# Expert positions of 112 slots, and silu in place of sigmoid and a product

## What is computed

```python
logits = (xf @ router_w + router_b)                 # 512 x 32
top_val, top_idx = lax.top_k(logits, 4)
gates = softmax(top_val)
# for each expert e, for the tokens routed to it:
gu = xb @ mlp1_w[e] + mlp1_b[e]                     # 1024 -> 2048
gate, up = gu[..., ::2], gu[..., 1::2]
gate = minimum(gate, 7.0)
up = clip(up, -7.0, 7.0)
act = (up + 1.0) * gate * sigmoid(1.702 * gate)
y = act @ mlp2_w[e] + mlp2_b[e]                     # 1024 -> 1024
out[token] += y * gates[token, e]
```

## Time and profile before

| | |
|---|---|
| time, median of 3 runs | 1603.47 us (1601.67 to 1604.37) |
| span of the profiled execution | 1602.2 us |
| TensorE matmul / weight load busy | 97% / 78% |
| VectorE / ScalarE / GpSimd busy | 82% / 67% / 22% |
| expert stage | from about 447 us to 1583 us |
| L1932, L1935, L1960, L1965 (expert matmuls) | 4608 matmuls, mean 389 to 399 ns |
| L1754 (`lo`) on VectorE | 384 x 2288 ns |
| L1618 (`hi`) on ScalarE | 384 x 1919 ns |
| DMA | 465 MB; 372 to 391 GB/s in most slices of the expert stage |

### The profile page before, as it was taken

The page is one execution under the profiler, slowest core; times in us unless marked ns, Lnnn a source line. Parts: engine busy times, 40 slices in busy tenths (PEclk is TensorE's granted clock), DMA queues, the critical chain, the costliest instruction groups (busy, mean ns, idle before and its releaser), DMA issues.

```text
span 1602.2 us, 27288 instructions
## 1 busy us (share of the span) xinstructions
PE 1547.4 (97%) x10197; PEld 1254.4 (78%) x10198; DVE 1320.1 (82%) x1101; ACT 1068.4 (67%) x1014; POOL 347.6 (22%) x278
## 2 busy tenths in 40 slices
PE   6899999987899999999999999999999999999997
PEld 5677777765778888888888888888888888888885
DVE  5556565656498999999999999999999999999996
ACT  4635353434367777777777777777777777777774
POOL 7100000001145322212222212222222222221210
PEclk9999999998999999999999999999999999999999
DMA  6211111006399999999999999999999999999993
GB/s 198 57 54 41 54 41 54 15 2 224 153 390 367 375 391 383 385 381 361 385 379 377 386 383 377 375 372 378 371 383 376 381 380 372 372 374 373 384 375 134
DMA packets 99101, 465.30 MB, mean 290 GB/s; under 512 B 11408, under 2 KB 38192, under 8 KB 49760
## 3 DMA queue, kind: packets, MB, share of 16 engines
q1 hardware_dynamic: 86176, 429.59, 68.7%
q0 software_dynamic: 12864, 34.85, 8.3%
HBM read 448.51 MB, written 22.69 MB: 294 GB/s over the span
## 4 chain that ended last, share of the span: by engine, by line
PE 73%; DVE 2%; DMA 1%; ACT 0%; issue 0%; DVEq 0%; POOLq 0%
PE psum L1932 29%; PE psum L1960 14%; PE psum L1935 14%; PE psum L1965 7%; PE psum L1330 3%; PE psum L1922 2%; PE psum L1914 2%; DVE w_pieces_lo L1754 1%; PE psum L1948 1%; DMA xg<-h_rows,gath_i 0%; DMA w_pieces<-in_mlp_w 0%; PE psum L1346 0%; PE psum L1338 0%; DVE x L1876 0%; DMA w_pieces<-in_w_out 0%
## 5 line engine op out<-in xcount | busy, mean ns | idle before, releaser
L1754 DVE TENSOR_TENSOR w_pieces_lo<-w_pieces,w_pieces_hi 128x2048 fp32r<-128x2048 f32 x384 | 867.6, 2288 | 79.8 <-ACT w_pieces_hi L1618 79.7
L1618 ACT ACTIVATE w_pieces_hi<-w_pieces 128x2048 fp32r<-128x2048 f32 x384 | 736.1, 1919 | 220.5 <-PE psum L1935 154.1
L1932 PE MATMUL psum<-w_pieces_hi,xh 128*128 128x512 f32 x1024 | 284.3, 399 | 0.0
L1932 PE MATMUL psum<-w_pieces_hi,xl 128*128 128x512 f32 x1024 | 274.4, 390 | 0.0
L1935 PE MATMUL psum<-w_pieces_lo,xh 128*128 128x512 f32 x1024 | 274.2, 389 | 0.0
L1558 POOL DMA_INDIRECT sum_rows<-ys,this_i x30 | 143.6, 4786 | 418.2 <-ACT ys L1638 417.9
L1932 PEld LDWEIGHTS psum<-w_pieces_hi,xl 128*128 128x128 f32 x1024 | 192.2, 188 | 41.3
L1935 PEld LDWEIGHTS psum<-w_pieces_lo,xh 128*128 128x128 f32 x1024 | 192.2, 188 | 40.3
L1932 PEld LDWEIGHTS psum<-w_pieces_hi,xh 128*128 128x128 f32 x1024 | 185.3, 188 | 45.1 <-issue 11.3
L1960 PE MATMUL psum<-w_pieces_hi,ah 128*128 128x512 f32 x512 | 158.0, 390 | 0.1
L1960 PE MATMUL psum<-w_pieces_hi,al 128*128 128x512 f32 x512 | 157.7, 389 | 0.0
(11 more groups left out here) (366 smaller groups left out, 1901.9 us busy)
## 6 DMA issues: line engine op xcount, KB each, us to landing
w_pieces<-in_mlp_w SPq DMA_DIRECT2D x384, 1024.0 KB, 8.0
w_raw<-in_w_in SPq DMA_DIRECT2D x26, 512.0 KB, 4.1
w_pieces<-in_w_out SPq DMA_DIRECT2D x8, 512.0 KB, 9.2
sum_rows<-x POOLq DMA_DIRECT2D x5, 512.0 KB, 3.7
chunk_work<-in_x SPq DMA_DIRECT2D x4, 512.0 KB, 6.1
sc<-pall POOLq DMA_DIRECT2D x16, 128.0 KB, 4.0
x<-in_x SPq DMA_DIRECT2D x4, 512.0 KB, 13.6
h_rows<-w_pieces POOLq DMA_DIRECT2D x4, 512.0 KB, 2.9
```

The lines of the kernel that those rows point to most:

```text
L1618: nc.scalar.activation(hi[:, p % RING], raw[:, raw_slot(b, p)].rearrange("p r n -> p (r n)"), ACT.Copy).then_inc(s_hi, 1)
L1754: nc.vector.tensor_tensor(lo[:, p % RING], raw[:, raw_slot(b, p)].rearrange("p r n -> p (r n)"), hi[:, p % RING].bitcast(F32), ALU.subtrac ...
L1932: nc.tensor.matmul(bank(up_bank(b) + c), a[:, k, :], hi[:, p % RING, c * 512:(c + 1) * 512], start=False, stop=False)
```

## The change

1. Slots. Experts are put at places. Place 0 is expert 0; place 1 is the expert with the most rows among 1 to 29, which changes places with expert 1. These two places have 128 slots, all others 112 (`NARROW`). In the matmuls of the narrow places the stationary operand has 112 columns, and PSUM gets 112 rows. The order is found out on VectorE at the end of `route_vector`; SyncE reads the expert of a place from SBUF into a register before it issues its loads, and `pick_bias` takes its column from a table built there. The lists are read in two DMAs, one for the wide places and one for the narrow. Rounds are five instead of four (a further one runs only if needed).
2. Activation. ScalarE computes silu(1.702 gate) in place of sigmoid(1.702 gate). The product min(gate, 7) x up of VectorE is gone, and `activate` takes min(silu, its value at 7). The factor 1/1.702 that is then missing is put into the gates.
3. On TensorE the turns 2 and 3 are written out ahead of the loop, since they work on a wide expert's down projection.

```diff
-INDEXED = EXPERTS + 2
+WIDE = 2
+NARROW = 112
+LAST_COL, RANK_COLS = 3, 5
...
-SIG_MAX = float(1.0 / (1.0 + np.exp(-1.702 * 7.0)))
-ROUNDS = S // P
+ALPHA = 1.702
+SILU_MAX = float(ALPHA * 7.0 / (1.0 + np.exp(-ALPHA * 7.0)))
+ROUNDS = -(-S // NARROW)
+LIST_ROWS = ROUNDS * P * EXPERTS
...
-        "pick": (p % EXPERTS) == np.arange(TURNS)[None, :],
+        "pick": (p % EXPERTS) == 0,
+        "lane": p % EXPERTS,
+        "among": np.broadcast_to(np.where((c >= 1) & (c < EXPERTS - 2), EXPERTS - 1.0 - c, -1e6)[:, :EXPERTS], (P, EXPERTS)),
+        "to_one": np.broadcast_to(1.0 - np.arange(EXPERTS)[None, :], (P, EXPERTS)),
+        "wide_first": np.broadcast_to((P - NARROW) * (np.arange(EXPERTS)[None, :] == 0), (P, EXPERTS)),
...
-        nc.vector.memset(rank[:], -1e6)
+        nc.vector.memset(pick_at[:], 0.0)
...
-        nc.vector.tensor_tensor(rank[:, :, 0:EXPERTS], hidden[:], ranks, ALU.add)
-        nc.vector.tensor_tensor(rank[:, :, INDEXED - 1:INDEXED], hidden[:, :, EXPERTS - 2:EXPERTS - 1], ranks[:, :, EXPERTS - 2:EXPERTS - 1], ALU.add)
-        chain(nc.vector.memset(r1[:, 29:30], 0.0))
+        nc.vector.tensor_tensor(rank_at[:, :, 0:1], hidden[:, :, 0:1], ranks[:, :, 0:1], ALU.add)
+        chain(nc.vector.tensor_tensor(rank[:], hidden[:], ranks, ALU.add))
...
-        chain(nc.vector.tensor_reduce(r1[:, 20:21], bank(5, NT * EXPERTS, (NT + 1) * EXPERTS), AX.X, ALU.max))
+        counts = bank(5, NT * EXPERTS, (NT + 1) * EXPERTS)
+
+        def over_tokens(a):
+            return a.rearrange("p (t e) -> p t e", t=1).to_broadcast([P, NT, EXPERTS])
+
+        chain(nc.vector.scalar_tensor_tensor(largest[:], counts, float(EXPERTS), con("among"), ALU.mult, ALU.add))
+        chain(nc.vector.tensor_reduce(r1[:, 21:22], largest[:], AX.X, ALU.max))
+        chain(nc.vector.tensor_scalar(only[:], largest[:], r1[:, 21:22], None, ALU.is_equal))
+        chain(nc.vector.tensor_tensor_reduce(moved[:], only[:], con("experts"), 1.0, 0.0, ALU.mult, ALU.add, r1[:, 22:23]))
+        chain(nc.vector.tensor_tensor(moved[:], only[:], con("to_one"), ALU.mult))
+        chain(nc.vector.tensor_tensor(place_of_expert[:], moved[:], con("experts"), ALU.add))
+        chain(nc.vector.tensor_copy(place_of_expert[:, 1:2], r1[:, 22:23]))
+        nc.vector.tensor_scalar(gates[:], gates[:], 1.0 / ALPHA, None, ALU.mult)
+        for place in range(1, 3):
+            last = nc.vector.scalar_tensor_tensor(at_place[:, place - 1], over_tokens(place_of_expert[:]), float(place), rank[:], ALU.is_equal, ALU.mult)
+        chain(last)
+        nc.vector.tensor_copy(expert_at[:], place_of_expert[:]).then_inc(g["s_order"], 1)
+        nc.vector.tensor_scalar(pick_at[:, 0:EXPERTS], place_of_expert[:], con("lane"), None, ALU.is_equal).then_inc(g["s_order"], 1)
+        nc.vector.tensor_reduce(rank_at[:, :, 1:3].rearrange("p t n -> p n t"), at_place[:], AX.X, ALU.add)
+        nc.vector.tensor_copy(rank_at[:, :, LAST_COL:RANK_COLS], rank[:, :, EXPERTS - 2:EXPERTS])
+        chain(nc.vector.scalar_tensor_tensor(largest[:], only[:], float(NARROW - P), counts, ALU.mult, ALU.add))
+        chain(nc.vector.tensor_tensor(largest[:], largest[:], con("wide_first"), ALU.subtract))
+        chain(nc.vector.tensor_reduce(r1[:, 20:21], largest[:], AX.X, ALU.max))
         for r in range(ROUNDS):
-            last = nc.vector.tensor_scalar(flags[:, r:r + 1], r1[:, 20:21], float(P * r) if r else -1.0, None, ALU.is_gt)
+            last = nc.vector.tensor_scalar(flags[:, r:r + 1], r1[:, 20:21], float(NARROW * r) if r else -1e6, None, ALU.is_gt)
...
-            src = down_rows(d, b - 2, p) if p < DOWN else gate_up_rows(d, b, p - DOWN)
+            src = down_rows(d, e, p) if p < DOWN else gate_up_rows(d, e, p - DOWN)
...
+            sp.wait_ge(g["s_order"], 1)
+            e = expert(1)
             for p in range(DOWN, PIECES):
-                load(r, 1, p)
+                load(r, 1, p, e)
             with sp.Fori(2, EXPERTS) as b:
-                for p in range(PIECES):
-                    load(r, b, p)
+                e = expert(b - 2)
+                for p in range(DOWN):
+                    load(r, b, p, e)
+                e = expert(b)
+                for p in range(DOWN, PIECES):
+                    load(r, b, p, e)
...
-            nc.gpsimd.dma_start(lists[:, 0:EXPERTS, :], g["list_dram"].rearrange("(r s e) w -> r s e w", s=P, e=EXPERTS)[bass.ds(r, 1)].rearrange(
-                "a s e w -> (a s) e w")).then_inc(s_lists, 16)
-            pool.wait_ge(s_lists, r * 16 + 16)
+            rows = g["list_dram"].rearrange("(s e) w -> s e w", e=EXPERTS)
+            nc.gpsimd.dma_start(lists[:, 0:WIDE, :], rows[bass.ds(r * P, P), 0:WIDE, :]).then_inc(s_lists, 16)
+            nc.gpsimd.dma_start(lists[0:NARROW, WIDE:EXPERTS, :], rows[bass.ds(r * NARROW, NARROW), WIDE:EXPERTS, :]).then_inc(s_lists, 16)
+            pool.wait_ge(s_lists, r * 32 + 32)
...
-            nc.scalar.activation(sg[:], pairs(e)[:, :, 0], ACT.Sigmoid, scale=1.702).then_inc(s_sig, 1)
+            nc.scalar.activation(sg[:], pairs(e)[:, :, 0], ACT.Silu, scale=ALPHA).then_inc(s_sig, 1)
...
-            nc.scalar.activation(pick[:], con("pick")[:, bass.ds(m, 1)].to_broadcast([P, P]), ACT.Copy).then_inc(s_pick, 1)
+            if not isinstance(m, int) or m:
+                act.wait_ge(g["s_order"], 2)
+            column = con("pick") if isinstance(m, int) and not m else pick_at[:, bass.ds(m, 1)]
+            nc.scalar.activation(pick[:], column.to_broadcast([P, P]), ACT.Copy).then_inc(s_pick, 1)
...
-        def gate_up(r, e, b, p):
-
+        def clip_up(r, e, b, p):
             dve.wait_ge(s_used, r * STREAM + (place(b, p) + 1 + RING))
-            nc.vector.tensor_scalar(uu[:], pairs(e)[:, :, 1], 8.0, -6.0, ALU.min, ALU.max).then_inc(s_u, 1)
-            dve.wait_ge(s_u, r * EXPERTS + (e + 1))
-            nc.vector.scalar_tensor_tensor(uu[:], pairs(e)[:, :, 0], 7.0, uu[:], ALU.min, ALU.mult).then_inc(s_x, 1)
+            nc.vector.tensor_scalar(uu[:], pairs(e)[:, :, 1], 8.0, -6.0, ALU.min, ALU.max).then_inc(s_x, 1)
...
-            nc.vector.scalar_tensor_tensor(av[:], sg[:], SIG_MAX, uu[:], ALU.min, ALU.mult).then_inc(s_act, 1)
+            nc.vector.scalar_tensor_tensor(av[:], sg[:], SILU_MAX, uu[:], ALU.min, ALU.mult).then_inc(s_act, 1)
...
+        def width(b):
+            return P if isinstance(b, int) and b < WIDE else NARROW
+
+        def rows_of(n, width):
+            return bank(n, 0, 512, slice(0, width))
...
-                    nc.tensor.matmul(bank(up_bank(b) + c), a[:, k, :], hi[:, p % RING, c * 512:(c + 1) * 512], start=False, stop=False)
+                    nc.tensor.matmul(rows_of(at + c, m), a[:, k, 0:m], hi[:, p % RING, c * 512:(c + 1) * 512], start=False, stop=False)
...
-                    nc.tensor.matmul(bank(up_bank(b) + 2 * half + c), pick[rows, :], bias[rows, c * 512:(c + 1) * 512], start=True, stop=False)
-            if isinstance(b, int):
+                    nc.tensor.matmul(rows_of(up_bank(b) + 2 * half + c, width(b)), pick[rows, 0:width(b)], bias[rows, c * 512:(c + 1) * 512], start=True, stop=False)
...
-                        nc.tensor.matmul(bank(into + c), a[:, 2 * p + r2, :], hi[:, p % RING, r2 * D + c * 512:r2 * D + (c + 1) * 512],
+                        nc.tensor.matmul(rows_of(into + c, m), a[:, 2 * p + r2, 0:m], hi[:, p % RING, r2 * D + c * 512:r2 * D + (c + 1) * 512],
...
-            with pe.Fori(2, EXPERTS) as b:
+            for b in range(2, 2 + WIDE):
+                down(r, b)
+                up(r, b, True)
+            with pe.Fori(2 + WIDE, EXPERTS) as b:
```

89 lines of the change are left out of this document (53 added, 36 removed).

## The result

The changed kernel takes 1616.2 us (median of 4 runs, 1615.44 to 1616.78), the kernel before 1603.34 us in the same comparison: ratio 1.0079, 95% interval 1.0067 to 1.0092. I had forecast 1605.9 and a range up to 1609.5. The profiled execution spans 1614.2 us instead of 1602.2: 12 us are to be found, and 2.4 were expected.

A forecast was written before the change was run, and what follows sets the result against it. The prediction took TensorE as setting the pace, with the DMA engines also full. Its terms, -0.8 + 2.3 + 0.9 = +2.4 us, took the profiled 1602.2 to 1604.6, plus 1.3 for the median: 1605.9 us, range 1598.0 to 1609.5.

The forecast's parts named there:

- The stationary width: TensorE, 4320 matmuls of the narrow experts: 112 columns instead of 128 change nothing, 0; bounds 0 and 13.3 ns saved each.
- Rivals B and C: TensorE matmuls: B, load steals from the stream, -7.2 us, chance 0.10; C, load and matmul set spacing, 57 us, 0.08.
- The uncovered loads: TensorE, two weight loads per expert at and after the bias pair, each 13.3 ns shorter: -0.8 us.
- Silu and the product: VectorE loses 1.22 us per expert and gains only idle time, ScalarE's activation keeps its cost: 0.
- the cover: Slack before TensorE reads the piece behind the lists, done by 519.4 and read at 521.33: 1.9 us.
- The lists: Slot lists in two DMAs: one more issue costs about 0.6 us, its landing overlaps the first: 0 on TensorE.
- Rival D: Third expert: the second list DMA lands after the first, TensorE stands 2.3 us, result 1608.2; chance 0.20.
- The routing chain: VectorE between `stacked` and `select(0, 1)`, ahead of its first split: 4.1 us more, of which +2.3 us arrive.
- The end: Kernel's end: each engine checks one more round's flag, 0 to 1.5 us, taken as +0.9 us.

The follow-up runs named there:

- b_w112: Kernel before with only the width changed: stationary operand and result rows 112 wide for the experts in the loop; 1611.22 us, ratio 1.0048.
- a_list1: Changed kernel with the slot lists read by one transfer of 128 rows instead of two; 1614.13 us, ratio 1.0065.
- b_silu: Kernel before with silu in place of sigmoid, one product fewer on VectorE and a small scaling of the gates; 1605.33 us, ratio 1.0010.
- b_product: Kernel before with silu in place of sigmoid and a value-neutral product put back on VectorE; 1604.44 us, ratio 0.9997.
- a_nochain: Changed kernel without its routing operations, the order of the experts being a constant; 1614.94 us, ratio 1.0078.
- b_guard: Kernel before with one look at the second round's flag on each engine enclosing the loop over later rounds; 1603.81 us, ratio 0.9998.
- a_turns_product: Changed kernel with 128-column products, one list transfer, narrow experts' transposes over 112 rows and columns, and a product put back on VectorE; 1605.06 us, ratio 1.0006.
- a_best: a_turns_product with the guard of b_guard, and the last routing operations and flags moved behind the slot lists; 1602.9 us, ratio 0.9996.

## Why the prediction was wrong, step by step

**The stationary width: the step that failed.** I took 0 for 4320 matmuls, with bounds of 0 and a gain of 13.3 ns. The reading behind it was right as far as it went: a matmul without a load above it takes what it takes with one, so the load doesn't lengthen the stream. But I turned it into "width doesn't touch the spacing" and let a cost below zero out of the bounds, though no row of the trace had a stationary width other than 128 in this stream. Measured: 1.9 ns more per matmul in the mean of an expert (229.2 to 231.1, without the two groups of transposes but with what follows them), 0.26 us per expert, +7.6 us. Rivals B and C had the sign wrong: both supposed that less work can only be faster. The Trainium skill ("TensorE: Matmul & The Clock Gate", section "Back-to-back issue gap") has the spacing set by both the load and the matmul, and I had dismissed that; the runs don't contradict it, but less load is not less time, for at 112 columns the load is 14 ns shorter and the spacing 2.2 ns longer. That the cost comes by way of the load isn't shown: each of these edits narrowed the load, the matmul's own stationary side and its PSUM rows together, and none took them apart. The matmul ahead of a bias group, which has no load above it, hints that it isn't the load alone: the prediction had its 388 ns stay, and it lasts 397 with 112 columns (after and b_w112), 388 with 128 and with 88.

**The uncovered loads: mis-sized.** Forecast -0.8. From the last matmul ahead of a bias group to the first behind it went from 979 to 975 ns, not by 27: the bias matmul starts 327 ns after the last one instead of 318, and only what follows is shorter. Some 0.1 us in all.

**Silu and the product: the steady part right, the cover wrong.** "What VectorE gains is idle time" held in each steady expert: VectorE's idle time ahead of `lo` grew from 79.8 to 124.8 us. I didn't ask what the freed VectorE would run into: GpSimd's issues in the first three experts, +0.95 us on the last scatter.

**The lists: the place right, the cause wrong.** Rival D named the third expert, 2.3 us, and that is what it cost (2.27), but the number agrees by luck: a_list1 shows that the second transfer is 0.2 of it. The list arrives 4.1 us later, in three parts: the scatters' end (0.95), the wait for the last one's landing (5.08 to 6.04 us) and the slower transfer (4.8 to 7.0 us). Less a cover of 1.7 us, which I had put at 1.9, that is 2.4. Only the first part is traced to the change, by b_silu and b_product. The landing took 4.6 to 6.2 us over the seventeen kernels, and why it and the transfer were slow here is open.

**The routing chain: size near, place wrong.** 4.1 us forecast, 3.4 measured. I followed it through VectorE's splits to the second bias group and took +2.3. It surfaces ahead of the first transposes, by 0.6 to 0.8 us. The first split came at 443.89 and the second bias group at 472.06, for 445 and 473.3 forecast.

The first expert's +0.78 is two things in the traces. Behind the first bias group the granted clock is at 0.50 (1.2 GHz) for 1.20 us before and 2.04 us after, about 0.4 us more at half speed. And at the expert's end TensorE waits 0.20 us for xl before, and 0.59 after:

```profile
472.06 0.73 PE L2007 MATMUL psum<-bias,pick_e 64*128 64x512 f32 x4 [0.59 <-DVE xl L1815]
```

Neither needs the chain. a_nochain has 1.31 us at 0.50 and waits 1.23 us (25.49 for the expert); b_silu has 4.42 us and no wait (25.68), and b_guard, with neither chain nor silu, 4.05 us and no wait (25.48). The eight other kernels without the chain took 24.3 to 24.6. What sets the length of either is open. Windows of TensorE (us, busy, clock, DMA share, GB/s), before and b_silu:

```profile
448.00:450.00 2.00, 2.00 (x10) 1.00 1.00 422
```

```profile
448.00:450.00 2.00, 2.00 (x6) 0.50 0.99 414
```

In the kernel before, the clock had been at 0.50 since 434.0, and TensorE was busy for 2.3 of the four us ahead of that; from there to the first expert it has short groups of matmuls with waits between them. It goes back to 1.00 some us into the first expert, 1.2 to 4.4 us behind the first bias group in the seventeen executions: before 448 in the one, after 450 in the other. At 0.50 the matmuls of the earlier trace rows are 427 ns apart.

**The end: right, with some luck.** Forecast +0.9, measured +0.95. The 0.9 was a middle between 0 and 1.5, and it is no price per check: two checks fewer gave 1.1 us (b_guard), three fewer 1.9 (5.57 to 3.66, a_turns_product to a_best).

In sum: about +1.1 for +2.3 up to the second bias group, of which 0.6 to 0.8 is traced to the chain, +0.95 for +0.9, 2.3 us for the lists where I had 0, and 7.7 us for the width, the uncovered loads within it, where I had -0.8.

## What to carry to other kernels

Work that is taken away still has to be followed: the freed engine starts its next operation earlier, beside something else. For an operand size that no row of the trace shows, leave both signs in the range, and try it alone before the bookkeeping that it needs is built: here 14 ns less per load made the stream slower, and b_w112, a few edited lines, would have told. Here fewer slots paid where they are moving columns (the transposes of x, 13 ns each), not where they are stationary ones.

## What the runs showed of the hardware

- The spacing of load and matmul pairs with 512 moving columns depends on the stationary width without order: 226.7 ns at 128, 127, 124 and 88 columns, 228 to 236 at the others tried, while the load gets 0.84 ns shorter per column. At 88 columns both 226.7 and 233.3 occur, by what ran before or by the place. What makes the step is open, and so is whether the load or the matmul's own width does it.
- A scatter issued by GpSimd takes 0.98 us beside a VectorE operation that reads PSUM, and ends 0.9 us after the end of a split with two SBUF inputs when it starts beside one: up to 3.1 us.
- A small transfer that reads 128 rows of the slot table, beside the stream of weight loads, took 3.9 to 5.6 us in the nine kernels that issued it by 37.8 us after the second bias group, and 5.9 to 7.1 in the eight that issued it between 38.0 and 39.8.
- One more check of a round's flag on all engines is 0.95 us at the end; two checks fewer were 1.1 us, three fewer 1.9.
- Behind the first bias group the granted clock stayed at 0.50 for 1.2 to 4.4 us, 1.2 to 4.1 in the eight kernels that are the same up to there, and the first expert took 25.5 to 25.7 us where it was over 4 us, against 24.3 to 24.6 in the eight kernels without the chain where it was 2.0 or less.
